# Streaming encoder step: 32 of the first tile's 128 value rows added by token on VectorE during the projection, and one projection chunk placed beside the first output product

## The reference, cut to what matters

```
h  = x + mixer(rmsnorm(x) @ w_in) @ w_out
xn = rmsnorm(h)                                   # per token, 1024 wide
eidx, g = top 16 of 128x128 keys, for 8 heads     # 128 experts per token, with gates g
act  = gelu(einsum('td,thkd->thk', xn, u_tab[eidx]))     # 128 dots of 1024 per token
out  = h + einsum('thk,thkd->td', g * act, v_tab[eidx])  # 128 weighted value rows per token
```

## Time and profile before

| | us |
|---|---|
| median of 3 runs | 4042.62 (4039.8 to 4049.7) |
| profiled execution, its own time | 4021.32 |
| its span, first to last instruction | 4019.0 |
| first tile's ids written | 307.5 |
| first dot of stage 0 begins | 361.9 |
| stage 0 ends (copy of the next tile's xn, L1805) | 729.5 |
| stage 1 ends | 1115.7 |

### The profile page before, as it was taken

One profiled execution on the slowest core, in us unless ns is written; L12 is line 12 of the kernel. 1 busy time (PEld: TensorE's weight loads), 2 busy tenths in 40 slices (PEclk: granted clock), 3 DMA queues, 4 the chain that ended last, 5 costly groups with the idle time before them and its releaser, 6 DMA issues.

```text
span 4019.0 us, 48466 instructions
## 1 busy us (share of the span) xinstructions
PE 2771.3 (69%) x16300; PEld 1398.7 (35%) x16300; DVE 2534.7 (63%) x6869; ACT 1059.4 (26%) x2881; POOL 2262.3 (56%) x2365
## 2 busy tenths in 40 slices
PE   6989999578568757775777487658874674333366
PEld 5845645343234324442443143315332331000011
DVE  2445657675877587758876787687677556544400
ACT  4312212332232323322332333233322111101121
POOL 1102443566666666655666666665666666666665
PEclk9989999778677867786778687868875675555567
DMA  7645798999999999999999999999999999999998
GB/s 205 192 131 167 260 335 275 343 383 377 383 374 371 393 381 375 369 383 360 379 372 382 372 370 378 390 384 347 377 381 362 376 391 352 370 375 361 366 372 315
DMA packets 545779, 1389.40 MB, mean 346 GB/s; under 512 B 61288, under 2 KB 225312, under 8 KB 545536
## 3 DMA queue, kind: packets, MB, share of 16 engines
q0 software_dynamic: 335024, 1215.35, 80.1%
q1 hardware_dynamic: 198288, 161.34, 12.6%
q10 hardware_dynamic: 12224, 9.63, 0.9%
HBM read 1352.93 MB, written 33.04 MB: 345 GB/s over the span
## 4 chain that ended last, share of the span: by engine, by line
PE 19%; DMA 15%; POOL 12%; DVE 10%; issue 10%; another core or an unknown queue 4%; ACT 1%; DVEq 0%; ACTq 0%; POOLq 0%
DMA d_vb<-in_peer_v_dram,d_eidT 7%; DMA d_ub<-in_peer_u_dram,d_eid 7%; PE d_pY L1756 6%; POOL d_vb L1726 6%; POOL d_ub L1707 5%; DVE d_ub L1920 4%; PE r_pB L1456 2%; PE d_pS L855 2%; PE d_pS L941 2%; PE d_pS L921 1%; PE r_pB L1471 1%; DMA d_ub<-in_peer_v_dram,d_eidT 1%; PE d_pS L880 1%; POOL d_ub L1726 1%
## 5 line engine op out<-in xcount | busy, mean ns | idle before, releaser
L1920 DVE CUSTOM_DVE_ANT_0 d_ub<-d_ub,d_pX 128x1024 f32<-128x1024 f32 x1024 | 1243.2, 1218 | 643.1 <-DMA d_ub<-in_peer_u_dram,d_eid 492.3
L1707 POOL DMA_INDIRECT d_ub<-in_peer_u_dram,d_eid x1152 | 1135.4, 986 | 890.1 <-DVE d_hdot L1920 396.5
L1756 PE MATMUL d_pY<-d_vb,d_dg 128*32 128x256 f32 x8768 | 961.4, 515 | 887.7 <-DMA d_vb<-in_peer_v_dram,d_eidT 581.4
L1726 POOL DMA_INDIRECT d_vb<-in_peer_v_dram,d_eidT x1096 | 1044.1, 953 | 722.6 <-PE d_pY L1756 262.0
L1756 PEld LDWEIGHTS d_pY<-d_vb,d_dg 128*32 128x32 f32 x8768 | 256.5, 128 | 1495.7 <-issue 1259.3
L1795 ACT ACTIVATE d_dg<-c_late_sb,d_wgtT 128x32 f32<-128x32 f32 x1152 | 335.8, 315 | 1248.6 <-PE d_pY L1756 735.3
L707 PE MATMUL d_pX<-d_wq,d_vb 128*128 128x512 f32 (+3 forms) x1536 | 470.1, 459 | 17.1 <-DMA d_vb<-in_w_in_dram 11.9
L707 PEld LDWEIGHTS d_pX<-d_wq,d_vb 128*128 128x128 f32 x1536 | 269.3, 199 | 181.7 <-issue 111.7
L1456 PE MATMUL r_pB<-r_side,c_small_sb 128*128 128x128 f32 (+15 forms) x1152 | 178.7, 325 | 19.2 <-DVE r_side L1385 10.1
L1456 PEld LDWEIGHTS r_pB<-r_side,c_small_sb 128*128 128x128 f32 x1152 | 178.2, 246 | 31.8 <-issue 17.2
L1920 DVE CUSTOM_DVE_ANT_0 d_ub<-d_ub,d_vb 128x1024 f32<-128x1024 f32 x128 | 155.6, 1225 | 48.7 <-DMA d_ub<-in_peer_u_dram,d_eid 47.9
(11 more groups left out here) (282 smaller groups left out, 3553.9 us busy)
## 6 DMA issues: line engine op xcount, KB each, us to landing
d_vb<-in_w_in_dram SPq DMA_DIRECT2D x68, 512.0 KB
d_ub<-in_peer_u_dram,d_eid POOLq DMA_INDIRECT x1152
d_vb<-in_peer_v_dram,d_eidT POOLq DMA_INDIRECT x1096
r_side<-in_cache_k_dram SPq DMA_DIRECT2D x16, 1024.0 KB
r_side<-in_cache_v_dram SPq DMA_DIRECT2D x16, 1024.0 KB
d_wo<-in_w_out_dram SPq DMA_DIRECT2D x6, 2048.0 KB, 9.1
d_wo<-in_peer_w_q_dram SPq DMA_DIRECT2D x4, 2048.0 KB, 8.7
scratch_h<-t_shared SPq DMA_DIRECT2D x9, 512.0 KB
```

The source lines that it names most:

```text
L1707: pool.indirect_dma_start(out=ub[:, g % R, :], out_offset=None, in_=io["peer_u"][0], in_offset=off).then_inc(u_in[g % R], 16)
L1726: pool.indirect_dma_start(out=to, out_offset=None, in_=io["peer_v"][0], in_offset=off).then_inc(landed, 16)
L1756: m = nc.tensor.matmul(pY[q * QT:(q + 1) * QT, g % 2, :], dg[:, n % DG, :], rows[:, q * QD:(q + 1) * QD], start=k % QT == 0, stop=k % QT = ...
L1920: nc.vector.tensor_tensor_reduce(out=ub[:, g % R, :], in0=ub[:, g % R, :], in1=xflat if i else xn_of(0), scale=1.0, scalar=0.0, op0=ALU.mu ...
```

## The change

**Values by token.** The first tile's experts are dotted in another order: numbers 96 to 127 first, then 0 to 95 (`FIRST_ORDER`). The gelu and the gates of those 32 follow at steps 36 and 38. From step 41 to 115, at 32 steps, GpSimd also gathers v rows by token (the same ring of 4, so 160 gathers go through it in stage 0), and VectorE adds weight x row to an accumulator that starts as `h`: half of it lies in PSUM (`pY`), half in the memory of `dg` and `wgtT` (two 128x512 SCALAR_TENSOR_TENSOR a row). The last of the 32 writes the sum into its own slot, and SyncE stores it as `h` of that tile. In stage 1 the v gathers of the first tile take 96 experts instead of 128 (96 rows on 96 partitions), and so do the matmuls.

**What waits for what now.** The store of the first tile's `h` moves from the output product to position 117, behind a wait for all 32 additions; the gather that reuses the last addition's slot waits for that store. TensorE's first product into `pY`, ScalarE's first `wgtT`, and `load_xs(0)` wait for the additions or the store.

**Positions.** The projection's chunk 40 moves from -86 to -112, where the first tile's output product begins (its products stand at -109 to -101, the transposes of xn at -98, the query product from -96). The last ten chunks at a pitch of 4.0 steps become nine at 4.4. Two semaphores are merged into others.

```
-    pos += [-86 + 8.5 * n for n in range(6)] + [-26] + [6.25 * n for n in range(8)] + [50 + 9.3 * n for n in range(3)]
-    pos += [78 + 4.0 * n for n in range(11)]
+    pos += [-112] + [-86 + 8.5 * n for n in range(6)] + [-26] + [6.25 * n for n in range(8)] + [50 + 9.3 * n for n in range(3)]
+    pos += [78 + 4.4 * n for n in range(10)]
...
+        own = [pY[:].rearrange("p a n -> p (a n)"), dgw[:, 0:512]]
...
             sp.wait_ge(h_done, i + 1)
-            sp.dma_start(sc["h"][t], x).then_inc(h_stored, 16)
+            if i:
+                sp.dma_start(sc["h"][t], x).then_inc(h_stored, 16)
...
+            if i == 1:
+                yield own_step[-1] + 2
+                sp.wait_ge(own_done, 2 * OWN)
+                rows, _, _ = own_slot(OWN - 1)
+                sp.dma_start(sc["h"][ORDER[0]], rows).then_inc(first_stored, 16)
...
+            if i == 0:
+                yield local(i, R0 + 16)
+                dve.wait_ge(c_near_done, 6)
+                for n in range(2):
+                    step(nc.vector.tensor_copy(own[n], x[:, 512 * n:512 * n + 512]))
...
+        OWN = NEXP - CUT
+        FIRST_ORDER = list(range(CUT, NEXP)) + list(range(CUT))
+        own_step = [41 + 12 * m // 5 for m in range(OWN)]
+        first_rows = sorted([(k, 0, k) for k in range(NEXP)] + [(k, 1, m) for m, k in enumerate(own_step)])
...
+                for a, (_, of_v, n) in enumerate(first_rows):
+                    if a >= R:
+                        _, last_v, last = first_rows[a - R]
+                        if last_v:
+                            pool.wait_ge(own_done, 2 * (last + 1))
+                            if last == OWN - 1:
+                                pool.wait_ge(first_stored, 16)
+                        else:
+                            pool.wait_ge(dot_done, last + 1)
+                    to, landed, _ = own_slot(n) if of_v else u_slot(n)
+                    k = CUT + n if of_v else FIRST_ORDER[n]
+                    pool.indirect_dma_start(out=to, out_offset=None, in_=io["peer_v" if of_v else "peer_u"][0], ...)
...
-                            off = bass.IndirectOffsetOnAxis(ap=eidT[:, (i - 1) % 3, k:k + 1], axis=0)
+                            some = CUT if i == 1 else P
+                            off = bass.IndirectOffsetOnAxis(ap=eidT[0:some, (i - 1) % 3, k:k + 1], axis=0)
...
+                        if i == 0 and k == OWN + 4:
+                            gelu(0, CUT, NEXP)
...
+                def add_own(m):
+                    rows, landed, count = own_slot(m)
+                    dve.wait_ge(landed, count)
+                    if m:
+                        dve.wait_ge(own_done, 2 * m)
+                    for n in range(2):
+                        half = rows[:, 512 * n:512 * n + 512]
+                        ins = nc.vector.scalar_tensor_tensor(own[n] if m < OWN - 1 else half, half, hdot[:, 0, CUT + m:CUT + m + 1], own[n],
+                                                             ALU.mult, ALU.add)
+                        ins.then_inc(own_done, 1)
...
+                        if i == 0 and k == OWN + 6:
+                            weigh(0, 0, CUT, NEXP)
+                            dve.wait_ge(wgt_done, 1)
+                        if i == 0 and k in own_step:
+                            add_own(own_step.index(k))
```

More of the change, by code:

```diff
@@ L1675, in layer, with u_slot, own_slot, gelus_before @@
         CUT = NEXP - 2 * PK
+        OWN = NEXP - CUT
+        FIRST_ORDER = list(range(CUT, NEXP)) + list(range(CUT))
+        own_step = [41 + 12 * m // 5 for m in range(OWN)]
+        first_rows = sorted([(k, 0, k) for k in range(NEXP)] + [(k, 1, m) for m, k in enumerate(own_step)])
+        at_first = {(of_v, n): a for a, (_, of_v, n) in enumerate(first_rows)}
+        def u_slot(g):
+            a = g + OWN if g >= NEXP else at_first[0, g]
+            return ub[:, a % R, :], u_in[a % R], 16 * (a // R + 1)
+        def own_slot(m):
+            a = at_first[1, m]
+            return ub[:, a % R, :], u_in[a % R], 16 * (a // R + 1)
+        def gelus_before(j):
+            return 2 * j + min(j, 1)
         with nc.Block() as block:
@@ L1697, in _ @@
                 pool.wait_ge(c_near_psum, 4 + 2)
-                for i in range(NT + 1):
+                pool.wait_ge(ids_done, 1)
+                for a, (_, of_v, n) in enumerate(first_rows):
[9 more added lines that the diff above has]
+                    k = CUT + n if of_v else FIRST_ORDER[n]
+                    pool.indirect_dma_start(out=to, out_offset=None, in_=io["peer_v" if of_v else "peer_u"][0],
+                                            in_offset=bass.IndirectOffsetOnAxis(ap=eid[:, 0, k:k + 1], axis=0)).then_inc(landed, 16)
+                for i in range(1, NT + 1):
                     for k in range(NEXP):
@@ L1752, in weigh_rows @@
                     g = k // QT
+                    some = P if j else CUT
                     if k % QT == 0 and 4 * j + g:
                         pe.wait_ge(h2_done, 4 * j + g)
+                    if n == 0:
+                        pe.wait_ge(own_done, 2 * OWN)
                     for q in range(4):
-                        m = nc.tensor.matmul(pY[q * QT:(q + 1) * QT, g % 2, :], dg[:, n % DG, :],
-                                             rows[:, q * QD:(q + 1) * QD], start=k % QT == 0, stop=k % QT == QT - 1)
+                        m = nc.tensor.matmul(pY[q * QT:(q + 1) * QT, g % 2, :], dg[0:some, n % DG, :],
+                                             rows[0:some, q * QD:(q + 1) * QD], start=k % QT == 0, stop=k % QT == QT - 1)
                     m.then_inc(exp_used, 1)
@@ L1852, in _ @@
                             if k == 0:
-                                gelu(j, CUT, NEXP)
+                                gelu(j, *((CUT, NEXP) if j else (CUT - OWN, CUT)))
                                 if i < NT:
@@ L1916, in _ @@
                             g = NEXP * i + k
-                            dve.wait_ge(u_in[g % R], 16 * (g // R + 1))
+                            rows, landed, count = u_slot(g)
+                            dve.wait_ge(landed, count)
                             if i and k == 0:
                                 dve.wait_ge(x_copied, i)
-                            nc.vector.tensor_tensor_reduce(out=ub[:, g % R, :], in0=ub[:, g % R, :], in1=xflat if i else xn_of(0), scale=1.0,
+                            c = k if i else FIRST_ORDER[k]
+                            nc.vector.tensor_tensor_reduce(out=rows, in0=rows, in1=xflat if i else xn_of(0), scale=1.0,
                                                            scalar=0.0, op0=ALU.mult, op1=ALU.add,
-                                                           accum_out=hdot[:, i % 2, k:k + 1]).then_inc(dot_done, 1)
+                                                           accum_out=hdot[:, i % 2, c:c + 1]).then_inc(dot_done, 1)
+                        if i == 0 and k == OWN + 6:
[3 more added lines that the diff above has]
+                            add_own(own_step.index(k))
                         main.until(NEXP * i + k)
```

52 lines of the change are left out of this document (29 added, 23 removed).

## The result

The changed kernel takes 4182.22 us (median of 5 runs, 4179.72 to 4197.75) against 4042.62 (4034.35 to 4049.7): a ratio of 1.0349 [1.033, 1.0368], 139.6 us slower. I had forecast 13 us faster. The slowest run of the kernel before is 130 us under the fastest of the changed one, so the sign is beyond doubt.

The account below looks back on a forecast made before the run. DMA engines were taken to set the pace from some 700 us on; of 30.5 us free behind step 41, 17 would stay free or be lost, a gain of 13: median 4042.6 to 4030, range 4008 to 4054.

Parts of the forecast that it names:

- What goes from stage 1: Stage 1's v gathers: a quarter of their rows, 16.8 MB or 43.8 us of DMA, goes; 41 us taken, bounds 0 and 44.
- Rival C: Stage 1's v gathers: 96 rows last as long as 128, the 41 us stay, 4070 us; chance 0.10.
- The rule that was weighed: Stage 1's v gathers: 96 partitions get 16 engines, each carrying six rows instead of eight, so the 43.8 us stand.
- the idle time of the DMA engines: Measure of the sum: 30.5 us free behind step 41, 17 left free or lost after the change, gain 13.
- Rival A: Up to 598 us in stage 0: a full DMA share isn't full rate, more gathers could lift it; 4009 us, chance 0.17.
- forecast 27: End of stage 0: 27 us later than 729.5, near 757, from the added gathers and waits.
- forecast 0.95 or more: Stage 0 from step 41 on: a DMA share of 0.95 or more as a sign that the forecast is right.
- forecast 1.5 us: VectorE's additions in stage 0: two instructions of 750 ns, 1.5 us a row, 48 us in all.
- forecast 14: TensorE's wait for VectorE at 512.43, before the output product: 14 us instead of 6.12.
- forecast 4 within 0 to 9: The new wait for the store near the projection's end: 4 us of idle DMA, bounds 0 and 9.
- The moved chunk: Chunk moved to the first output product: 6 us of TensorE products, first ids 2 us later, bounds 0 and +6.
- the work taken from the end of stage 0: End of stage 0: 6 us of TensorE and 2.5 us of DMA leave; with the store of `h`, net -1.1 us of DMA.

Follow-up runs that it names:

- e1: The changed kernel, but stage 1 gathers all 128 value rows again (matmuls still use 96): 3854.35 against 3835.71 us, ratio 1.0048.
- e2: The kernel before with only the first tile's stage 1 value gathers cut to 96 rows, the other experts left out: 3976.08 us, ratio 1.0369.
- e4: A kernel of gathers alone, eight slots, row counts varied, layer not computed: 1.44 us for 128 rows, 1.65 for 96.
- e8: Gathers alone, varying how many are in flight and where rows lie: with eight slots, 128 and 128 rows 2.72 us a pair, 128 and 96 3.53.
- e12: Gathers alone, bytes against partitions, some with two slots: a pair of 128 rows of 4 KB and 128 of 2 KB took 2.61 us.
- e6: The kernel before with the new chunk positions alone: 3824.35 against 3833.03 us, ratio 0.9968.
- e5: The changed kernel with stage 1's 128 gathers of 96 value rows packed into 96 of 128: 3831.93 against 3833.03 us, ratio 0.999.
- e7: The changed kernel with the old chunk positions and all 128 rows in stage 1's value gathers: 3862.83 us, ratio 1.0068.
- e9: The kernel before, unchanged, profiled in a single execution on the second experiment chip: 3840.24 us.

## Why the prediction was wrong

**The step that failed** is "What goes from stage 1": 41 us less, bounded by 0 and 44. The stage got 119.5 us longer. I took a gather of 96 rows to cost three quarters of one of 128, because the queue's time in the earlier trace rows goes by megabytes. But all gathers in those rows have 128 rows; they can't tell a price by bytes from a price by gathers, and say nothing of what other shapes cost. My lower bound, 0, was a bound on a saving. Nothing in the rows excluded a loss, and I should have let the bound go below nothing. e1 (loss gone with 128 rows) and e2 (the same loss in the kernel before) show that the row count alone does it. Apart from the layer a pair of 128 and 96 rows took 3.87 us in e4, against the stage's 3.95 a step, and 3.53 and 3.43 in e8 and e12; a pair of full gathers took 2.72 (e8). Over 128 steps that is a loss of 91 to 104 us in e8 and e12 and, against twice a full gather's 1.44, of 127 in e4; the stage lost 119.5.

**Rival C** had the right place and the right sign, and a price that was too small: it let a 96-row gather last as long as one of 128 and ended at 4070. Of its signs "stage 1 over 375 us, GB/s down by an eighth" the first held, and the rate fell by a third (379 to 257).

**The rule that was weighed** (the Trainium skill, DMA: Bandwidth & Descriptors, section "Why a DMA increments its semaphore by 16 and not by 1") says that 96 partitions get 16 engines. The share of 1.03 agrees, all of them are busy; only the conclusion from it, six rows an engine in three quarters of the time, was mine, and the runs contradict it: with eight slots in flight 96 rows took 1.65 us, not three quarters of 1.44.

**The share as a measure.** The prediction counted the idle time of the DMA engines, "since their work stays the same". A share says that packets are under way, not how fast they go: 1.03 at 257 GB/s and 1.02 at 393 stand side by side (after, e1). Rival A had said this of the earlier trace rows, but I used it in one direction only.

**What held, in stage 0.** Its end came 33.8 us later, forecast 27, with the share of 0.96 from step 41 on (forecast 0.95 or more). A row's addition took 754 + 746 ns, forecast 1.5 us. TensorE waited 10.7 us before the output product, forecast 14. GpSimd waited 7.9 us for the store, forecast 4 within 0 to 9. Not foreseen: TensorE waits 19.7 us for VectorE at 748, on the way to the second tile's ids, where it waited 2.8 before; what it cost no run shows.

**The moved chunk.** I read the row of eight products at 259.58 as a whole segment; it is half of one. The code has eight products a segment, but the trace holds each as two records: 1536 in all, for 768 products. TensorE around the first output product after the change:

```profile
218.29 5.52 PE L708 MATMUL d_pX<-d_wq,d_vb 128*128 128x512 f32 x8 [0.51 <-issue]
224.94 3.70 PE L928 MATMUL d_pS<-d_wo,d_mT 128*128 128x512 f32 x8 [0.69 <-ACT d_mT L1025]
233.62 3.60 PE L708 MATMUL d_pX<-d_wq,d_vb 128*128 128x512 f32 x8
242.21 2.74 PE L708 MATMUL d_pX<-d_wq,d_vb 128*128 128x384 f32 x8
259.37 2.74 PE L708 MATMUL d_pX<-d_wq,d_vb 128*128 128x384 f32 x8
```

The chunk is 2 x 3.60 + 2 x 2.74 = 12.7 us, not 6. Two of its four parts lie behind TensorE's old waits. The ids came 5.3 us later in e6, near the upper bound of 6, not 2. The upper clock level was half foreseen: the chunk's first part runs at a granted clock of 0.65 (5.52 us), and the output product behind it at 1.00 (3.70 us). In the kernel before the same product ran at 0.57, its four transposes included:

```profile
217.13 6.17 PE L921 MATMUL d_pS<-d_wo,d_mT 128*128 128x512 f32 x8 [0.69 <-ACT d_mT L1018]
```

In all, the positions brought 0.3% (e6), 9 us by the medians and 12 by the ratio, where my terms came to about nothing. The term that was mis-sized is the work taken from the end of stage 0, 12.7 us of TensorE and not 6, but that this is where the gain comes from I can't show: the stages give 1.3 + 4.4 + 3.9, and that is single profiled executions against each other.

**If the mechanism had been right.** e5 is the change as it was meant, its saving intact, but for some more work of ScalarE (139.6 us in stage 1 instead of 113). Stage 0 pays 36.4 us (761.2 against 724.8), stage 1 gives 33.9 over the kernel before, 32.3 over e7 and 26.4 over e1. By the runs this version isn't told from the kernel before, and its ratio is 0.2% over e6's, the positions alone; the two intervals just overlap, near 0.998. So even with the price that I had taken, values by token in this form would have brought no gain that these runs can see. Two terms were mis-sized there: stage 0's 27, and the 41, of which 7 to 15 us are missing where I had kept 3 for VectorE. That VectorE's dots at 83% and the ring of four take them is likely by GpSimd's longer wait for free slots (74.5 us against 48.4 in e1), but no run changed either alone. The lowest median of all that ran is e6's, 3824.35 us, 0.2 to 0.45% under the kernel before.

**What stays open** is why a full queue slows down short gathers. The expectations name mechanisms; the rows fit none of them whole. What is shown: the slowdown depends on how many partitions a gather has, on which ones, and on how many are in flight (there with eight, gone with one and two). That the DMA engines get unequal shares of rows and collide on the way to the same memory is a guess; no view here tells which engine wrote which partition.

## What to carry to other kernels

Keep gathers at the full 128 partitions where many are in flight: pack what is left into fewer full gathers instead of trimming each, and measure a shape that the trace doesn't contain before its cost goes into a sum. Bound an unseen operation on the side of loss too, and read the DMA share only together with the GB/s beside it. Work that is moved into a stage pays back only what is free at its own positions, and the stage that it leaves may find its next limit (here probably VectorE and its ring) before the whole saving is taken.

## What the runs showed of the hardware

- With eight slots in flight gathers of 4 KB rows took, each, 1.44 us for 128 rows, 2.17 for 120, 1.81 for 112, 1.65 for 96 and 1.37 for 64 (e4); at one in flight 4.47 for 128, 4.53 for 112, 4.30 for 96 and 3.98 for 64 (e8).
- With two in flight a pair of 128 and 96 rows took 4.56 us, one of 128 and 128 5.23, both at 201 GB/s (e12).
- GpSimd issued a gather in 0.95 us and began the next 0.30 later, 1.25 us in all (e4); the fastest mixed phases of 64 gathers took 81.7 to 83.5 us (e8, e12), 1.28 to 1.30 a gather, though their bytes and places differ.
- The kernel before took 4042.6 us where the result was measured and 3833 to 3836 on the two chips of the experiments; stage 1's rate was 379 and (e9) 391 GB/s, the first ids came at 307.5 and 305.4.
- TensorE's first eight 128x512 matmuls of the output product took 6.17 us behind a wait of 3.87 us and four transposes (granted clock 0.57, partly at the lower level), and 3.70 us behind eight other matmuls of 5.52 us (1.00, the upper level).
